# Scaling the exponentials before they are turned, in the attention of a twelve-stage block kernel

## The chip, the cores and the metric

The kernel runs on one core of one Trainium2 chip. The metric is the device time of one execution in microseconds; a kernel is judged by the median of its runs. Engines are called PE (TensorE), ACT (ScalarE), DVE (VectorE), POOL (GpSimd) and SP (the queue that issues most DMA transfers).

## The reference, cut to what matters

Two stacks of layers run one after the other on 512 latent tokens of width 1024 (the second stack also has 256 context tokens). Three layers hold a softmax attention with heads of 64 values:

```python
def fox(q, k, v, F):          # 16 heads, causal, 512 tokens: forgetting attention
    s = q @ k.T / 8 + (F_i - F_j)            # masked above the diagonal
    o = softmax(s) @ v
    return (o * silu(u @ w_z)) @ w_out
def even_mixer(...):          # layer with the "mla" attention, 8 heads, 768 keys
    y_lat = concat([a_lat, b_lat], -1) @ w_out       # b_lat = softmax(q k) v
def odd_mixer(...):           # two attentions of 8 heads each
    p = softmax(concat([s_loc, s_ctx], -1))          # "na": a window and the context, 512 keys
    d_lat = blocked_attention(qd_l, ...)             # "gqa": 768 keys
    y_lat = concat([c_lat, d_lat], -1) @ w_out
```

All is float32. A large product is made as three products of rounded halves (high x high, high x low, low x high), so each operand is needed as a "high" part (rounded copy) and a "low" part (the rest), and the left operand is needed with its features on the partitions.

## The kernel before, in words

Each engine runs a program of its own, in the order in which the functions `pe_...`, `act_...`, `dve_...` issue it; they are tied by counting semaphores (`A`, `V`, `B` are those of ACT, DVE and PE; `wait_ge(*V.of(name))` waits until DVE has done what is called `name`). Each engine runs its instructions strictly in this order, so an instruction that waits holds back all behind it. `X.chain()` waits for the engine's own last instruction.

An attention is a list of units: one head and one tile of 128 queries, with `nk` keys. Units go in pairs n, n+1. The three functions `pe_attention`, `act_attention` and `dve_attention` run over the pairs in a pipeline. In the iteration of pair n, PE does: the transposes of the exponentials of unit n-2 (`turned`, L902), the scores of n and n+1 (L893), the transposes of unit n-1, the transpose of the result of pair n-4 (`output`, L924), and the products of pair n-2 with the values (`values`, L917). ACT copies a turned unit from PSUM (`probs`, L955), makes the exponentials with their sum (`softmax`, L969, in the trace an ACTIVATE and a short ACTIVATION_READ_ACCUMULATOR behind it) and copies the pair's result (`out_copy`, L978). DVE copies the other turned unit (L1002; in fox and na, where a mask or bias is added to the scores, ACT copies both), inverts the two sums (L1006), takes the maxima of the next scores (L1023, behind the mask or bias, L1464 and L2937), and scales the turned results of pair n-4 by the inverse sums (`done`, L1031).

There are five such loops: fox (64 units: 16 each with 128, 256, 384 and 512 keys), mla in two groups (24 units each: 16 with 768 keys, 8 with 256), gqa (32 units, 768 keys) and na (32 units, 512 keys). In fox, at n = 0, 8, ..., 48, PE first runs a "side chunk" (`pe_chunk`, L558, 32 products with a modulation weight); at n = 48 ACT and DVE also split the next weights into high and low (L349 and L356, two instructions each), DVE between its maxima of pair 48 and those of pair 50. In the first mla group DVE runs two gating operations of another result (`beside`, L2754 and L2757) behind its maxima in each of the first six iterations.

The values product leaves a pair's result as features x tokens; `out_copy`, `output` and `done` turn it into tokens x features. After fox the gate z is made in tokens (`pe_linear_tok`), and the result is multiplied by it. Then every layer end (`pe_first_end`, `pe_second_end`) turns its input back into features (`pe_to_feat`, L710: 32 transposes, 48 in the even layer), ACT takes the high part (L729) and DVE the low part (L739), PE spreads a gate vector over the partitions (`pe_gate`, L756), and `pe_end` runs the output product (L400 to L402).

## Time and profile before

| | |
|---|---|
| median of 3 runs (lowest to highest) | 3508.91 us (3508.07 to 3514.5) |
| the profiled execution: its time, its span | 3506.47 us, 3504.7 us |
| PE busy | 3195.7 us (91% of the span) |
| DVE, ACT, POOL busy | 1706.0 us (49%), 1220.5 us (35%), 284.6 us (8%) |
| DMA | 301.32 MB, mean 86 GB/s |

The span is that of the profiled execution from its first to its last instruction. An engine's busy share is an average over all stages; it doesn't say which engine ends the waits in one of them. The attention loops lie at about 722 to 861 us (fox), 1895 to 1962 and 1996 to 2061 us (mla), 2887 to 2979 us (gqa) and 2980 to 3053 us (na).

### The profile page before, as it was taken

The numbers are of one execution on the slowest core, as the hardware profiler recorded it, in microseconds if no ns is written. First come the engines' busy times: TensorE is split into PE (matmuls) and PEld (weight loads), VectorE is DVE, ScalarE is ACT, GpSimd is POOL, SyncE is SP. The second block draws the span as 40 slices with busy tenths as digits, with TensorE's granted clock in tenths as the row PEclk, the third lists the DMA queues.
The fourth block names the chain that finished last, engine by engine and source line by source line (L and its number), as shares of the span: only waits on it lengthen the run. The fifth ranks groups of instructions, "written<-read, shape, count | busy, mean of one in ns | idle before, by whom it ended". The sixth has DMA issues, their size and how long they took to land.

```text
span 3504.7 us, 55559 instructions
## 1 busy us (share of the span) xinstructions
PE 3195.7 (91%) x23754; PEld 2597.7 (74%) x23754; DVE 1706.0 (49%) x2816; ACT 1220.5 (35%) x2195; POOL 284.6 (8%) x284
## 2 busy tenths in 40 slices
PE   6988988998999799899998789999999888889998
PEld 4767767755777687788886568888887775578886
DVE  3255435445433556667765545333334346644344
ACT  3325324346341465322224444211112425642221
POOL 0020010000002000133330000000000101000000
PEclk9999999989999999899998999999999989999999
DMA  5282222272224122132121001212121313013221
GB/s 203 92 299 88 96 97 73 99 282 77 74 81 168 59 71 75 55 109 76 63 71 41 25 1 45 74 64 72 49 72 52 92 50 72 1 44 113 96 97 72
DMA packets 164064, 301.32 MB, mean 86 GB/s; under 512 B 9606, under 2 KB 30919, under 8 KB 163561
## 3 DMA queue, kind: packets, MB, share of 16 engines
q1 hardware_dynamic: 148064, 278.71, 23.3%
q10 hardware_dynamic: 13641, 11.55, 1.0%
q0 software_dynamic: 2112, 7.50, 0.8%
q8 instruction: 187, 3.06, 0.4%
q14 instruction: 60, 0.49, 0.0%
HBM read 289.62 MB, written 6.76 MB: 85 GB/s over the span
## 4 chain that ended last, share of the span: by engine, by line
PE 76%; DVE 15%; ACT 6%; issue 1%; DMA 1%; POOL 0%; ACTq 0%; DVEq 0%; SPq 0%; POOLq 0%
PE psum L400 17%; PE psum L401 17%; PE psum L402 17%; PE psum L2278 5%; PE psum L893 4%; PE psum L917 3%; PE psum L902 3%; PE psum L558 2%; DVE weights_r L356 2%; DVE arena L816 1%; DVE x_lat L819 1%; PE psum L2342 1%; PE psum L2350 1%; DVE feat_r L739 1%; PE psum L756 1%
## 5 line engine op out<-in xcount | busy, mean ns | idle before, releaser
L356 DVE TENSOR_TENSOR weights_r<-weights,weights_r 128x2048 fp32r<-128x2048 f32 (+2 forms) x170 | 368.3, 2188 | 551.9 <-ACT weights_r L349 551.7
L400 PE MATMUL psum<-feat_r,weights_r 128*128 128x512 f32 (+1 forms) x1552 | 544.6, 351 | 14.7 <-DVE feat_r L697 12.4
L400 PE MATMUL psum<-weights_r,feat_r 128*128 128x512 f32 (+2 forms) x1344 | 531.5, 395 | 23.7 <-DVE feat_r L697 14.9
L401 PE MATMUL psum<-feat_r,weights_r 128*128 128x512 f32 (+1 forms) x1552 | 542.8, 350 | 0.0
L402 PE MATMUL psum<-feat_r,weights_r 128*128 128x512 f32 (+1 forms) x1552 | 542.0, 349 | 0.0
L402 PE MATMUL psum<-weights_r,feat_r 128*128 128x512 f32 (+2 forms) x1344 | 524.3, 390 | 0.0
L401 PE MATMUL psum<-weights_r,feat_r 128*128 128x512 f32 (+2 forms) x1344 | 524.3, 390 | 0.0
L349 ACT ACTIVATE weights_r<-weights 128x2048 fp32r<-128x2048 f32 (+2 forms) x170 | 306.5, 1825 | 600.9 <-DMA weights<-in_w_ffn_gate 224.9
L400 PEld LDWEIGHTS psum<-feat_r,weights_r 128*128 128x128 f32 x1552 | 296.1, 191 | 58.4 <-DVE feat_r L697 12.8
L402 PEld LDWEIGHTS psum<-feat_r,weights_r 128*128 128x128 f32 x1552 | 296.0, 191 | 37.9
L401 PEld LDWEIGHTS psum<-feat_r,weights_r 128*128 128x128 f32 x1552 | 296.1, 191 | 37.4
L400 PEld LDWEIGHTS psum<-weights_r,feat_r 128*128 128x128 f32 x1344 | 258.7, 192 | 75.6 <-DVE feat_r L697 15.8
L402 PEld LDWEIGHTS psum<-weights_r,feat_r 128*128 128x128 f32 x1344 | 257.6, 192 | 51.5
L401 PEld LDWEIGHTS psum<-weights_r,feat_r 128*128 128x128 f32 x1344 | 258.6, 192 | 49.0
L400 PE MATMUL psum<-weights_r,arena_r 128*128 128x512 f32 x440 | 173.5, 394 | 10.0 <-DVE arena L1834 6.2
L401 PE MATMUL psum<-weights_r,arena_r 128*128 128x512 f32 x440 | 172.1, 391 | 0.0
L402 PE MATMUL psum<-weights_r,arena_r 128*128 128x512 f32 x440 | 172.0, 391 | 0.0
L675 POOL CAST feat_r<-feat 128x512 fp32r<-128x512 f32 x76 | 49.1, 646 | 1393.5 <-ACT feat L667 1393.5
L1023 DVE TENSOR_REDUCE small<-psum 128x1 f32<-128x768 f32 (+4 forms) x176 | 121.7, 691 | 32.1 <-PE psum L893 22.4
L667 ACT ACTIVATE feat<-psum,small 128x128 f32<-128x128 f32 x304 | 109.0, 480 | 27.3 <-PE psum L636 24.2
L558 PE MATMUL psum<-weights,cond 128*32 128x512 f32 x768 | 100.5, 669 | 13.7 <-DVE feat L2496 8.6
L400 PEld LDWEIGHTS psum<-weights_r,arena_r 128*128 128x128 f32 x440 | 83.1, 189 | 30.5 <-DVE arena L1834 6.4
(472 smaller groups left out, 4587.2 us busy)
## 6 DMA issues: line engine op xcount, KB each, us to landing
weights<-in_w_mod SPq DMA_DIRECT2D x48, 2048.0 KB, 12.6
weights<-in_gla_w_in SPq DMA_DIRECT2D x24, 1024.0 KB, 7.4
weights<-in_w_ffn_gate SPq DMA_DIRECT2D x20, 1024.0 KB, 6.3
weights<-in_w_ffn_up SPq DMA_DIRECT2D x20, 1024.0 KB, 5.1
weights<-in_w_ffn_down SPq DMA_DIRECT2D x20, 1024.0 KB, 6.2
weights<-in_fox_w_in SPq DMA_DIRECT2D x16, 1024.0 KB, 6.8
weights<-in_sgu_w_in SPq DMA_DIRECT2D x12, 1024.0 KB, 6.2
weights<-in_gla_w_out SPq DMA_DIRECT2D x8, 1024.0 KB, 6.6
```

The costliest lines, as they stand in the source:

```text
L349: act.e.activation(WEI_r[:, s * SLOT + HALF:s * SLOT + HALF + n], WEI_t[:, s * SLOT:s * SLOT + n], ACT.Copy).then_inc(*A.put(("weights", c ...
L356: dve.e.tensor_tensor(WEI_r[:, s * SLOT:s * SLOT + n], WEI_t[:, s * SLOT:s * SLOT + n], WEI_r[:, s * SLOT + HALF:s * SLOT + HALF + n].bitc ...
L400: pe.e.matmul(ps, lh, rh, start=first, stop=False)
L401: pe.e.matmul(ps, lh, rl, start=False, stop=False)
L402: done = pe.e.matmul(ps, ll, rh, start=False, stop=last)
L558: done = pe.e.matmul(ps[32 * j:32 * j + 32, :], cond_at(mod, k, b), where[k][0], start=b == 0 and k < 4, stop=b == 1 and k >= 4)
L667: act.e.activation(FL_plain[:, k, t * P:(t + 1) * P], K.at[at][:, m * P:(m + 1) * P], ACT.Identity, bias=PRE_B[:, c0 + k:c0 + k + 1], scal ...
L893: done = pe.e.matmul(ps[m][:, n0:n0 + w], lt, rh, start=first, stop=last)
L902: done = pe.e.transpose(ps[:, j * P:(j + 1) * P], PR[n % 3][:, j * P:(j + 1) * P], ident)
L917: done = pe.e.matmul(ps[half, 0:P], units[m]["values"][j], PTR[m % 2][:, j * P:(j + 1) * P], start=j == 0, stop=j == last)
L1023: dve.e.tensor_reduce(NEGM[:, i:i + 1], src, AX.X, ALU.max, negate=True).then_inc(*V.put((tag, "max", n)))
L2278: done = pe.e.matmul(out_[rows, (h - heads[0]) * 64:(h - heads[0] + 1) * 64], lhsT[rows, h, :], rhs[rows] if len(rhs.shape) == 2 else rhs[ ...
```

## The change

**In the loops.** DVE no longer scales results. Behind each exponential it inverts the sum and multiplies the 128 x nk exponentials by it in place (`scaled`), and PE's transposes of that unit wait for this instead of for the exponential. The values product then leaves the final result, with features on the partitions; `out_copy` writes it straight to its place, and `output`, `done` and the extra iteration for them are gone. The four attention destinations (`to`) are now features x tokens.

**At the ends.** What comes from an attention isn't transposed any more; ACT and DVE split it row by row (`act_row`, `dve_row`: a row is 128 features x all tokens). After fox, z is made by features, and gate, high and low of row m follow each product; the gate vector's spreading moves into the z product. In the even layer four of eight rows still come over transposes, and ACT alternates between these and rows. In the odd layer there are eight rows and no transposes. `pe_end` waits row by row.

```diff
@@ pe_product: takes ks, the order of its terms; ready(k) is called ahead of term k @@
-    def pe_product(pe, c, ps, terms, names, ready=None):
+    def pe_product(pe, c, ps, terms, names, ready=None, ks=range(KT)):
...
+    def act_row(act, tag, k, high, y):
+
+        act.chain()
+        act.e.activation(high, y, ACT.Copy).then_inc(*A.put((tag, "high row", k)))
+
+    def dve_row(dve, tag, k, low, y, high):
+        dve.wait_ge(*A.of((tag, "high row", k)))
+        dve.e.tensor_tensor(low, y, high.bitcast(F32), ALU.subtract).then_inc(*V.put((tag, "row", k)))
...
@@ pe_end @@
+                def ready(k, t=t):
+                    pe.wait_ge(*V.of((tag, "row", k) if k in by_k else (tag, "feat", t, k // 4)))
...
@@ pe_attention @@
-            pe.wait_ge(*A.of((tag, "exp", n)))
+            pe.wait_ge(*V.of((tag, "scaled", n)))
...
-        def output(n):
-            pair = n // 2
-            pe.wait_ge(*A.of((tag, "out", pair)))
-            pe.e.transpose(K.at[(tag, "values", pair)][:, P:2 * P], out_t[pair % 2],
-                           ident).then_inc(*B.put((tag, "output", pair)))
...
@@ act_attention @@
-                act.wait_ge(*V.of((tag, "done", n - 6)))
+                act.wait_ge(*V.of((tag, "scaled", n - 6)))
...
+            at = (tag, "values", n // 2)
             act.wait_ge(*B.of((tag, "values", n)))
...
+            act.e.activation(units[n]["to"], K.at[at][:, 0:P], ACT.Copy).then_inc(*A.put(K.frees(A, at), (tag, "out", n // 2)))
...
@@ dve_attention @@
+        def scaled(n):
+
+            nk, total = units[n]["nk"], SUM[:, n % 6:n % 6 + 1]
+            dve.wait_ge(*A.of((tag, "exp", n)))
+            dve.chain()
+            dve.e.reciprocal(total, total).then_inc(*V.put())
+            dve.chain()
+            dve.e.tensor_scalar(PR[n % 3][:, 0:nk], PR[n % 3][:, 0:nk], total, None, ALU.mult).then_inc(
+                *V.put((tag, "scaled", n)))
...
-            dve.wait_ge(*A.of((tag, "exp", n)))
-            dve.chain()
-            dve.e.reciprocal(SUM[:, n % 6:n % 6 + 1], SUM[:, n % 6:n % 6 + 1]).then_inc(*V.put((tag, "inverse", n)))
...
-        def done(n):
...
         last = len(units)
-        for n in range(0, last + 4, 2):
-            if 2 <= n < last + 2:
+        for n in range(0, last + 2, 2):
+            if n >= 2:
+                scaled(n - 2)
+                scaled(n - 1)
                 probs(n - 2)
                 probs(n - 1)
...
@@ pe_fox: z by features, with the gate vector after its block 4 @@
-        pe_linear_tok(pe, (T, "z"), feat_tile, KT, "fox_w_in", 3072, 1024, LAT)
+        pe_linear_feat(pe, (T, "z"), "fox_w_in", 3072, 1024, [(0, 512)],
+                       after={((T, "z"), 4, 0): lambda: pe_gate(pe, ("end", 2), 0)})
...
@@ act_fox @@
+            act.e.activation(f_zs[m % 2], K.at[at], ACT.Silu).then_inc(*A.put(K.frees(A, at), (T, "z", m)))
+            act.wait_ge(*V.of((T, "gated", m)))
+            act_row(act, ("end", 2), m, f_H[:, m, :], f_qT[:, m, :])
...
@@ dve_fox @@
+            dve.e.tensor_tensor(f_qT[:, m, :], f_qT[:, m, :], f_zs[m % 2], ALU.mult).then_inc(*V.put((T, "gated", m)))
+            dve_row(dve, ("end", 2), m, f_L[:, m, :], f_qT[:, m, :], f_H[:, m, :])
...
@@ act_second_end @@
+        if i == 0:
+            act_to_feat(act, T, tiles, halves=(0,), between=lambda t: row(4 + t) if t < 4 else None)
+        else:
+            act.wait_ge(*B.of((W_, "na")))
+            for k in second_rows[1]:
+                row(k)
...
@@ dve_second_end @@
+        if i == 0:
+            dve_to_feat(dve, T, tiles, halves=(0,))
+            dve.wait_ge(*B.of((T, "turned")))
+        for k in second_rows[i]:
+            y, high, low = second_row(i, k)
+            dve_row(dve, T, k, low, y, high)
```

**The order on the engines.** DVE in the gqa loop before, from the maxima of one pair to the scaling of an older one:

```order
1563 L1023 TENSOR_REDUCE small<-psum 128x1 x2
1564 L1002 COPY feat<-psum 128x768
1565 L1006 RECIPROCAL small<-small 128x1 x2
1566 L1023 TENSOR_REDUCE small<-psum 128x1 x2
1567 L1031 TENSOR_SCALAR arena<-psum,small 128x64 x2
```

And DVE at the same place now:

```order
1749 L1027 TENSOR_REDUCE small<-psum 128x1 x2
1750 L997 RECIPROCAL small<-small 128x1
1751 L999 TENSOR_SCALAR feat<-feat,small 128x768
1752 L997 RECIPROCAL small<-small 128x1
1753 L999 TENSOR_SCALAR feat<-feat,small 128x768
1754 L1009 COPY feat<-psum 128x768
```

Two scalings over 768 elements stand ahead of the copy of the turned unit and of the maxima; two small ones behind the maxima are gone.

ACT from the last pair of the mla attention to the gates of the even layer's end, before:

```order
805 L955 ACTIVATE arena<-psum 128x256
806 L978 ACTIVATE arena<-psum 128x128
807 L729 ACTIVATE feat_r<-psum 128x4x128 x12
808 L765 ACTIVATE arena<-psum 128x512 x4
809 L349 ACTIVATE weights_r<-weights 128x2048 x2
```

And now:

```order
819 L976 ACTIVATE arena<-psum 128x128
820 L721 ACTIVATE feat_r<-psum 128x4x128
821 L739 ACTIVATE feat_r<-arena 128x768
822 L721 ACTIVATE feat_r<-psum 128x4x128
823 L739 ACTIVATE feat_r<-arena 128x768
824 L721 ACTIVATE feat_r<-psum 128x4x128
825 L739 ACTIVATE feat_r<-arena 128x768
826 L721 ACTIVATE feat_r<-psum 128x4x128
827 L739 ACTIVATE feat_r<-arena 128x768
828 L721 ACTIVATE feat_r<-psum 128x4x128 x2
829 L767 ACTIVATE arena<-psum 128x512 x4
```

Six of twelve high parts from PSUM became four longer ones from SBUF, which stand between the others.

DVE from the last unit of the na attention to the next weights in the odd layer's end, before:

```order
1717 L1031 TENSOR_SCALAR arena<-psum,small 128x64 x4
1718 L739 TENSOR_TENSOR feat_r<-psum,feat_r 128x4x8x16 x4
1719 L739 TENSOR_TENSOR feat_r<-psum,feat_r 128x4x128 x4
1720 L747 TENSOR_TENSOR small<-mod_cols,param_cols 128x8
1721 L681 SCALAR_TENSOR_TENSOR small<-mod_cols,param_cols 128x8
```

And now:

```order
1911 L997 RECIPROCAL small<-small 128x1
1912 L999 TENSOR_SCALAR feat<-feat,small 128x512
1913 L743 TENSOR_TENSOR feat_r<-arena,feat_r 128x512 x8
1914 L749 TENSOR_TENSOR small<-mod_cols,param_cols 128x8
1915 L682 SCALAR_TENSOR_TENSOR small<-mod_cols,param_cols 128x8
```

The low parts stay eight instructions of 512 elements, ahead of the gate vector (L749) for which PE waits; they read SBUF now and no transposes stand ahead of them.

## Rows read from the trace of the kernel before

**Rows 1.** The page's chain of work that ended last, shares of the span by engine

```profile
PE 76%; DVE 15%; ACT 6%; issue 1%; DMA 1%; POOL 0%; ACTq 0%; DVEq 0%; SPq 0%; POOLq 0%
```

**Rows 2.** Timeline of one gqa pair: start and length in us, engine, line, what

```profile
2900.84 0.90 ACT L969 ACTIVATE feat<-psum,small 128x768 f32<-128x768 f32 x1
2901.64 0.19 ACT L969 ACTIVATION_READ_ACCUMULATOR feat<-psum,small 128x1 f32 x1
2902.26 0.87 PE L902 MATMUL psum<-const,feat 128*128 128x128 f32 x6
...
2904.24 0.43 DVE L1006 RECIPROCAL small<-small 128x1 f32<-128x1 f32 x2
...
2906.37 0.90 ACT L969 ACTIVATE feat<-psum,small 128x768 f32<-128x768 f32 x1
```

**Rows 3.** Timeline of one na pair

```profile
3015.16 0.69 ACT L969 ACTIVATE feat<-psum,small 128x512 f32<-128x512 f32 x1
...
3015.42 0.69 DVE L1023 TENSOR_REDUCE small<-psum 128x1 f32<-128x512 f32 x1
...
3015.75 0.19 ACT L969 ACTIVATION_READ_ACCUMULATOR feat<-psum,small 128x1 f32 x1
...
3016.24 0.66 PE L902 MATMUL psum<-const,feat 128*128 128x128 f32 x4
```

**Rows 4.** Timeline of one fox pair with 512 keys

```profile
847.84 0.69 ACT L969 ACTIVATE x_ctx<-psum,small 128x512 f32<-128x512 f32 x1
...
848.91 0.66 PE L902 MATMUL psum<-const,x_ctx 128*128 128x128 f32 x4
```

**Rows 5.** Timeline of one pair of the first mla group

```profile
1908.62 2.02 DVE L1023 TENSOR_REDUCE small<-psum 128x1 f32<-128x768 f32 x2 [0.40 <-PE psum L893]
...
1910.61 0.90 ACT L969 ACTIVATE feat<-psum,small 128x768 f32<-128x768 f32 x1
...
1911.38 0.69 DVE L2754 TENSOR_TENSOR feat<-feat,arena 128x512 f32<-128x512 f32 x1
...
1912.03 0.87 PE L902 MATMUL psum<-const,feat 128*128 128x128 f32 x6
```

**Rows 6.** Timeline in fox behind the side chunk of n = 48

```profile
822.96 4.48 DVE L356 TENSOR_TENSOR weights_r<-weights,weights_r 128x2048 fp32r<-128x2048 f32 x2
...
825.69 1.11 PE L902 MATMUL psum<-const,x_ctx 128*128 128x128 f32 x4
```

**Rows 7.** Groups by line and form on DVE: count, busy us, mean ns

```profile
L691 DVE TENSOR_SCALAR arena<-x_lat,small 128x1024 f32<-128x1024 f32 x32 | 24.1, 754 | 1.1
...
L2129 DVE TENSOR_SCALAR arena<-arena 128x128 f32<-128x128 f32 x6 | 1.7, 283 | 0.0
```

**Rows 8.** Timeline of PE from fox's z product to its output product

```profile
904.99 0.39 PE L402 MATMUL psum<-weights_r,feat_r 128*128 128x512 f32 x1
...
916.11 0.77 PE L400 MATMUL psum<-weights_r,feat_r 128*128 128x512 f32 x1
```

**Rows 9.** Timeline of the even and the odd layer's end

```profile
2060.85 0.60 DVE L1031 TENSOR_SCALAR arena<-psum,small 128x64 f32<-128x64 f32 x2 [1.12 <-PE psum L924]
2061.51 4.32 PE L710 MATMUL psum<-const,feat 128*128 128x128 f32 x24 [0.70 <-DVE arena L1031]
...
2071.43 5.45 PE L756 MATMUL psum<-const,small 128*128 128x128 f32 x32 [2.98 <-DVE small L747]
...
3062.05 2.05 PE L756 MATMUL psum<-const,small 128*128 128x128 f32 x16 [2.32 <-DVE small L747]
```

**Rows 10.** Timeline of PE where gqa ends and na begins

```profile
2979.79 0.33 PE L924 MATMUL psum<-const,feat 128*128 128x128 f32 x1 [0.38 <-ACT feat L978]
...
2983.48 1.11 PE L902 MATMUL psum<-const,feat 128*128 128x128 f32 x4 [2.29 <-ACT feat L969]
```

**Rows 11.** Windows in na: stretch, us, busy us of PE, PEld, DVE, ACT, POOL, PEclk, DMA, GB/s

```profile
2994.62:3048.05 53.43, 44.74 (x429) 32.72 (x429) 39.68 (x105) 39.34 (x92) 0.00 (x0) 1.00 0.01 2
...
2983.00:2993.00 10.00, 8.74 (x44) 6.12 (x44) 3.35 (x9) 4.83 (x12) 0.00 (x0) 0.50 0.00 0
```

More of the change, by code:

```diff
@@ L699, in dve_low, with pe_to_feat @@
                                 ALU.subtract).then_inc(*V.put((pre, "feat", t)))
-    def pe_to_feat(pe, tag, y, tiles):
+    def pe_to_feat(pe, tag, y, tiles, halves=(0, 1)):
         pe.wait_ge(*A.of((tag, "in")))
         pe.wait_ge(*V.of((tag, "in")))
-        for h in range(2):
+        for h in halves:
             for t in tiles:
@@ L777, in pe_end @@
                 ends = [("weights", c)] if t == tiles[-1] else []
-                pe_product(pe, c, ps, [(feat_tile(k, t), where[k]) for k in range(KT)], [(tag, n0, t)] + ends)
+                def ready(k, t=t):
+                    pe.wait_ge(*V.of((tag, "row", k) if k in by_k else (tag, "feat", t, k // 4)))
+                pe_product(pe, c, ps, [(src(k, t), where[k]) for k in ks], [(tag, n0, t)] + ends, ready, ks)
                 if n0 and beside[j] is not None:
@@ L972, in out_copy @@
         def out_copy(n):
-            pair = n // 2
+            at = (tag, "values", n // 2)
             act.wait_ge(*B.of((tag, "values", n)))
-            if pair >= 2:
-                act.wait_ge(*B.of((tag, "output", pair - 2)))
             act.chain()
-            act.e.activation(out_t[pair % 2], K.at[(tag, "values", pair)][:, 0:P],
-                             ACT.Copy).then_inc(*A.put((tag, "out", pair)))
+            act.e.activation(units[n]["to"], K.at[at][:, 0:P], ACT.Copy).then_inc(*A.put(K.frees(A, at), (tag, "out", n // 2)))
         last = len(units)
-        for n in range(0, last + 4, 2):
+        for n in range(0, last + 2, 2):
             if att_side(n, sides):
                 act_side(act)
-            if 2 <= n < last + 2:
+            if n >= 2:
                 probs(n - 2)
@@ L1023, in softmax @@
             dve.e.tensor_reduce(NEGM[:, i:i + 1], src, AX.X, ALU.max, negate=True).then_inc(*V.put((tag, "max", n)))
-        def done(n):
-            pair = n // 2
-            at = (tag, "values", pair)
-            dve.wait_ge(*B.of((tag, "output", pair)))
-            for m in (n, n + 1):
-                dve.chain()
-                dve.e.tensor_scalar(units[m]["to"], K.at[at][:, P + 64 * (m % 2):P + 64 * (m % 2) + 64],
-                                    SUM[:, m % 6:m % 6 + 1], None,
-                                    ALU.mult).then_inc(*V.put(K.frees(V, at), (tag, "done", m)))
         last = len(units)
-        for n in range(0, last + 4, 2):
-            if 2 <= n < last + 2:
+        for n in range(0, last + 2, 2):
+            if n >= 2:
+                scaled(n - 2)
+                scaled(n - 1)
                 probs(n - 2)
@@ L2725, in program @@
     m_att = [FEAT_t[:, 6144 + n * 768:6912 + n * 768] for n in range(4)] + [ar(3072, 768)]
-    m_out = [ar(3840 + n * P, P) for n in range(2)]
     M_ = ("mla",)
@@ L3152, in pe_second_end @@
             pe_gate(pe, T, v)
-        pe.wait_ge(*V.of((T, "feat")))
-        pe_end(pe, T, name, tiles, ("preffn", i))
+        pe_end(pe, T, name, tiles, ("preffn", i), ks=list(range(KT)) if i == 0 else second_rows[1], by_k=second_rows[i])
         pe_ffn(pe, i, tiles)
```

157 lines of the change are left out of this document (79 added, 78 removed).

## The prediction

> **What bounds the kernel now.** I read the page's chain first: three quarters of the end time hang on PE [rows 1]. The change touches five attention loops and three layer ends, so what counts is which wait ends last inside one pair. In gqa [rows 2] the first exponential of a pair starts at 2900.84 and its accumulator row ends at 2901.64 + 0.19 = 2901.83. PE turns that unit at 2902.26, and the next pair's exponential starts at 2906.37: 5.53 us a pair. Between them PE does the next scores (they must stand behind the transposes in its program), then the second unit's transposes, ACT copies these and only then makes the next exponential. So it is one ring: exponential, transposes, scores, transposes, copy, exponential. From the exponential's end to the transposes only 0.43 us pass. In na the ring goes over the maxima; from the exponential's start to the transposes are 3016.24 - 3015.16 = 1.08 us [rows 3], and 13 pairs take 53.43 us, 4.11 each [rows 11]. Fox with 512 keys has 848.91 - 847.84 = 1.07 us there [rows 4], mla 1.42 like gqa [rows 5]. The reader is to see that nothing stands between exponential and transposes that could be taken away: PE comes nearly as soon as the exponential is done. DVE, on the other hand, is idle at that moment, and its reciprocals (0.43 us for two [rows 2]) and its scaling of results lie outside the ring.
>
> **What the change adds: a stop at DVE in the ring.** Each unit's transposes now wait for reciprocal and scaling. The parts:
>
> - A hand-over between engines: DVE's last scaling ends at 2060.85 + 0.60 = 2061.45 and PE starts at 2061.51 [rows 9]. I take 0.05 us each, from ACT to DVE and from DVE to PE.
> - Reciprocal to the next instruction that depends on it: 0.43 us for two, each 0.16, so 0.27 from start to start [rows 2].
> - The scaling itself, S. It isn't in this trace at these sizes. A multiply of SBUF by a column of scalars takes 754 ns at 1024 elements, another TENSOR_SCALAR from SBUF 283 ns at 128 [rows 7]; a line through both gives 0.49 us at 512 and 0.62 at 768. The bound from above is one element per cycle, as in a maximum over 768 from PSUM, 2.02 / 2 = 1.01 us [rows 5], or about 0.34 more at 768 and 0.25 at 512. A bound from below is no gain over the line, less 0.05. I take the line, since its upper row is the same operation with the same kinds of operands.
>
> The Trainium skill, "VectorE: DVE Perf Modes", "Mode 2×_2P — use both read ports for one tensor", says that an operation with one tensor input, SBUF on both sides, makes two results a cycle even in float32; rows 7 agree, and by that rule the sum is the one below, by the PSUM row about 20 us more.
>
> From the accumulator's end to the transposes it was 0.43 us in gqa and is now 0.05 + 0.27 + 0.62 + 0.05 = 0.99: **+0.56 us a pair** in gqa, and in mla's long pairs. In fox at 512 keys it was 0.29 (the accumulator's end is 0.78 behind the start [rows 3]) and becomes 0.37 + 0.49 = 0.86: **+0.57**; I take this for all fox pairs, as shorter units have a shorter scaling but had less slack. In na the maxima of the second unit end at 3015.42 + 0.69 = 3016.11, 0.95 behind the exponential's start and later than its accumulator; the reciprocal stands behind them in DVE's order, so the transposes come at 0.95 + 0.05 + 0.27 + 0.49 + 0.05 = 1.81 instead of 1.08: **+0.73**. Only the pair's first unit counts; the second's transposes stand behind the scores, which leave DVE over 1.5 us for it.
>
> Sum of the loops:
>
> - fox, 32 pairs. Six of the waits fall under a side chunk, which PE runs first. One (behind n = 48) is dearer: the scaling stands behind the weight splits, which end at 822.96 + 4.48 = 827.44, so PE turns at about 828.4 and not at 825.69 [rows 6], +2.7. The other 25 cost 25 x 0.57 = 14.3. Together 17.0.
> - mla: 16 long pairs x 0.56 = 9.0; 8 short ones about 0.5 each, 4.0. In the first group the two gating operations (0.69 each [rows 5], about 1.45 with gaps) now start when the maxima end, which is when the next exponential starts (1908.62 + 2.02 = 1910.64 against 1910.61), and hold DVE until 1.45 behind it, while the accumulator ends at 0.99: +0.45 five times, and 1.45 in the first iteration, where nothing else hides them: 3.7. Together 16.7.
> - gqa: 16 x 0.56 = 9.0. na: 16 x 0.73 = 11.7.
>
> Together **+54.4 us**.
>
> **What it takes away.** DVE's scaling of results and PE's `output` lie in idle time of both, so in the middle of a loop they give nothing. At a loop's end PE no longer waits for copy and transpose: 0.38 idle and 0.26 until the next scores [rows 10], about 0.65; this counts for fox, the first mla group and gqa, -2.0. At fox's end, PE went from its last z product (904.99 + 0.23) to the output product at 916.11 [rows 8]: 10.9 us. Now each row's gate, high and low run under the next row's 24 products, and the last row (Silu, multiply, copy, subtract, some 2.8 us) is ready before the first output product comes to its eighth term, 7 x 0.68 = 4.8 us in. What stays is the gate vector, about 2.0 us at PE's full clock [rows 9]: **-8.9**.
>
> In the even layer's end, the transposes no longer stand behind `output` (0.33 [rows 10]) and DVE's two scalings (0.60) with their hand-overs, so they start about 1.0 earlier, at 2060.5 [rows 9], and the first high part a good microsecond behind that, at 2061.6. ACT then alternates: six highs of 0.62 and four rows over 768, priced like the exponential's 0.90 [rows 2], 7.3 us, the sixth high ending at 2068.9. DVE takes the low parts of all six tiles first and then four rows of about 1.0, so it ends 4.7 later, at 2073.6, and the two gate vectors reach PE at about 2074.0 and not at 2071.43: **+2.6**. In the odd layer's end eight low parts stand ahead of the gate vector as before, without the lead of the transposes; PE's gate products start some 2 us before 3062.05, but behind a longer idle stretch, so at the low clock, which takes back half: **-1**, an estimate.
>
> **Sum:** 54.4 - 2.0 - 8.9 + 2.6 - 1.0 = +45.1 us. The profiled execution took 3506.5 us, 2.4 under the median of the three runs, so this gives 3551.6; against the median it would be 3554. I say 3552, 1.3% slower.
>
> **Rivals.**
>
> - *PE's clock falls.* The new waits add idle time to PE at every pair. At the start of na, after 2.29 us of idling [rows 10], the granted clock was 0.50 (1.2 GHz) for ten microseconds, and 1.00 (2.4 GHz) in the steady part with PE busy 44.74 of 53.43 us [rows 11]. With 0.73 more idle in 4.84 that busy share falls from 84% to 72%. At the low clock four transposes take 1.11 instead of 0.66 us [rows 10, 3]; scaled to all PE work of a pair, 3.44 us, of which part is hidden, a na pair is some 2 us longer: +32 if all of na stays low, and some +8 to +15 for the short pairs of fox and mla. The time would be 3570 to 3595. Against it: the gaps are under 1.5 us each and PE works in between. The Trainium skill, "TensorE: Matmul & The Clock Gate", "Part 1: The HAM clock gate (the "warmup" mystery)", says that the slow clock is the default and activity lifts it; by that rule a thinner loop can fall back, and the na start in the rows is such a case.
> - *The scaling runs at one element a cycle.* 32 long pairs x 0.34, 16 na pairs and the longer half of fox x 0.25, about 20 us more: 3572. Against it stands the 754 ns row.
> - *The ring has slack that I don't see* (half of each wait goes under something, or hand-overs are shorter): +0.25 to 0.4 a pair, 3525 to 3538.
> - *Faster: the stop at DVE is hidden.* Place: PE's transposes of each pair's first unit. If PE were still at the values product of the older pair when the scaling ends, the loops would cost nothing and the ends would give 2.0 + 8.9 - 2.6 + 1.0 = 9.3: 3497. There are 80 pairs on the ring (25 + 24 + 16 + 15 or 16), so this decides below 9.3 / 80 = 0.12 us a pair. In gqa PE's transposes follow the exponential by 0.43 us, of which PE's own older work can explain 0.38 at most if a hand-over is 0.05, and the stop is 0.99 long. Little speaks for it.
>
> **How the numbers follow.** The forecast, 3540 to 3560, has 0.5. The clock rival 0.2, slow scaling 0.08, hidden slack 0.16, the faster case 0.06. The range 3530 to 3590 takes in the bounds of S and most of the clock rival, and leaves out the faster case, the lower half of the slack case and the clock's extreme: 0.8 inside. A change under 0.2% can't be told from none here. Faster 0.06, same 0.02, slower 0.92.
>
> **What would show it.** In the changed kernel: gqa pairs of about 6.1 us (5.53 before), na 4.84 (4.11), a TENSOR_SCALAR of 0.62 us at 768, PE's transposes released by DVE and not by ACT; fox's output product straight behind the z product; PE's gate products in the even layer 14 us behind the last values product. Wrong would be unchanged pair times, or na pairs above 6 us with a granted clock of 0.50.

## The result, and the profile after

The changed kernel takes 3566.23 us (median of 4 runs, 3562.88 to 3567.17), the kernel before beside it 3508.49 us: ratio 1.0163, 95% interval 1.0148 to 1.0178, so 1.6% slower. The profiled execution took 3562.88 us with a span of 3561.1 us; before it was 3506.47 and 3504.7, so the traces differ by 56.4 us. The page after, busy time by engine and the chain that ended last (answers to [rows 1]):

```profile
PE 3196.0 (90%) x23578; PEld 2590.2 (73%) x23578; DVE 1746.7 (49%) x2814; ACT 1222.8 (34%) x2193; POOL 285.1 (8%) x284
...
PE 73%; DVE 17%; ACT 7%; issue 1%; DMA 1%; POOL 0%; ACTq 0%; DVEq 0%; SPq 0%; POOLq 0%
```

PE's busy time is as before, and DVE has won in the chain: the new work is done by an engine that was idle half the time, and the end comes later all the same. Where it comes later, by the starts of the same instructions in both traces:

| stretch | before, us | after, us | difference | in the prediction's sum |
|---|---|---|---|---|
| start to fox's first exponential | 725.77 | 726.92 | +1.15 | 0 |
| to the first z product | 135.83 | 158.49 | +22.66 | +16.35 |
| to fox's output product | 54.51 | 45.48 | -9.03 | -8.9 |
| to mla's first exponential (code unchanged) | 980.16 | 982.56 | +2.40 | 0 |
| both mla groups, to the even end's gate products | 175.16 | 191.03 | +15.87 | +18.65 |
| to gqa's first exponential (code unchanged) | 816.22 | 816.10 | -0.12 | 0 |
| to na's first exponential | 95.00 | 107.26 | +12.26 | +8.35 |
| to the odd end's output product | 81.21 | 90.56 | +9.35 | +10.7 |
| to the end (code unchanged) | 440.84 | 442.70 | +1.86 | 0 |

A gqa pair after, which answers to [rows 2] (start and length in us):

```profile
2963.92 0.90 ACT L968 ACTIVATE feat<-psum,small 128x768 f32<-128x768 f32 x1
2964.72 0.19 ACT L968 ACTIVATION_READ_ACCUMULATOR feat<-psum,small 128x1 f32 x1
2964.95 0.16 DVE L997 RECIPROCAL small<-small 128x1 f32<-128x1 f32 x1 [0.72 <-ACT feat L968]
...
2965.14 0.62 DVE L999 TENSOR_SCALAR feat<-feat,small 128x768 f32<-128x768 f32 x1
...
2965.82 0.88 PE L909 MATMUL psum<-const,feat 128*128 128x128 f32 x6 [0.41 <-DVE feat L999]
...
2969.93 0.90 ACT L968 ACTIVATE feat<-psum,small 128x768 f32<-128x768 f32 x1
```

The accumulator row ends at 2964.91. Before, PE's transposes came 0.43 us behind that; now reciprocal and scaling stand between, and PE starts at 2965.82, 0.91 behind it, released by DVE. The next pair's exponential starts 6.01 us behind this one's. A na pair, for [rows 3]:

```profile
3059.82 0.69 ACT L968 ACTIVATE feat<-psum,small 128x512 f32<-128x512 f32 x1
...
3060.07 0.69 DVE L1027 TENSOR_REDUCE small<-psum 128x1 f32<-128x512 f32 x1
...
3060.86 0.16 DVE L997 RECIPROCAL small<-small 128x1 f32<-128x1 f32 x1
3061.06 0.49 DVE L999 TENSOR_SCALAR feat<-feat,small 128x512 f32<-128x512 f32 x1
...
3061.61 0.66 PE L909 MATMUL psum<-const,feat 128*128 128x128 f32 x4 [0.64 <-DVE feat L999]
...
3064.64 0.69 ACT L968 ACTIVATE feat<-psum,small 128x512 f32<-128x512 f32 x1
```

The maxima end at 3060.76, the reciprocal starts 0.10 later, and PE comes at 1.79 us behind the exponential instead of 1.08; the pair takes 4.82 us. The scalings of mla, gqa and na (minimum, median and maximum in ns), for [rows 7]:

```profile
L999 DVE TENSOR_SCALAR feat<-feat,small x112: 352/619/4487, 1914.9 to 3105.2; 128x768 f32<-128x768 f32 x64, 128x512 f32<-128x512 f32 x32, 128x256 f32<-128x256 f32 x16
```

The two pairs above have 0.62 us at 768 keys and 0.49 at 512, as the prediction's line through two groups said. But the maximum is 4487 ns. Around it, GpSimd, DVE and PE in gqa:

```profile
2943.48 14.10 POOL L2999 TENSOR_TENSOR feat<-feat,arena 128x2048 f32<-128x2048 f32 x3 [134.62 <-DMA feat<-rpb_spans]
...
2948.72 4.49 DVE L999 TENSOR_SCALAR feat<-feat,small 128x768 f32<-128x768 f32 x1
...
2953.32 0.96 DVE L1009 COPY feat<-psum 128x768 f32<-128x768 f32 x1
...
2954.33 1.54 PE L909 MATMUL psum<-const,feat 128*128 128x128 f32 x6 [3.48 <-DVE feat L1009]
```

GpSimd's three additions over 128 x 2048 (the bias of the neighbourhood attention) happened to run under gqa. The scaling at 2948.72 lasts 4.49 us instead of 0.62, PE stands idle for 3.48 us, and its next transposes run at the low clock (1.54 us for six, 0.88 above). Two gqa pairs took 10.51 and 7.11 us in place of 6.01, 5.6 us together. Before, the additions ran under the same loop, where DVE only read PSUM and inverted sums. Its TENSOR_SCALAR from PSUM kept its 0.60 us for two beside them, and every gqa pair behind the first took 5.53:

```profile
2907.85 13.49 POOL L2997 TENSOR_TENSOR feat<-feat,arena 128x2048 f32<-128x2048 f32 x3 [133.71 <-DMA feat<-rpb_spans]
...
2912.43 0.60 DVE L1031 TENSOR_SCALAR arena<-psum,small 128x64 f32<-128x64 f32 x2
```

In fox the clock took part. Windows over the whole loop, first before, then after with two pieces of it (stretch, us, busy us of PE, PEld, DVE, ACT and POOL, PEclk, DMA share, GB/s):

```profile
725.80:861.60 135.80, 118.64 (x939) 67.63 (x939) 79.83 (x264) 83.53 (x232) 0.00 (x0) 0.91 0.57 204
```

```profile
726.90:885.40 158.50, 125.64 (x906) 68.69 (x906) 87.09 (x267) 83.29 (x232) 0.00 (x0) 0.84 0.49 175
762.00:779.00 17.00, 14.28 (x79) 7.12 (x82) 8.75 (x31) 7.71 (x26) 0.00 (x0) 0.60 0.52 193
785.80:802.00 16.20, 12.50 (x107) 6.86 (x109) 9.76 (x33) 9.24 (x29) 0.00 (x0) 1.00 0.71 251
```

At 1.00 a pair with 256 keys takes 3.35 us (2.71 before); in the piece from 762 to 779, mostly at 0.50 (1.2 GHz), 4.39 to 4.48. All in all 51.2 us of the fox loop lie at the low level, 23.9 before.

### The profile page after: what moved, and what is told of

Read it like the earlier page. It is cut to its first block, busy times and chain, and to the rows that moved or that the text cites. A ratio compares the mean times of both kernels' runs of the same rounds, so it can differ in the third digit from the quotient of the medians.

```text
span 3561.1 us, 55142 instructions
## 1 busy us (share of the span) xinstructions
PE 3196.0 (90%) x23578; PEld 2590.2 (73%) x23578; DVE 1746.7 (49%) x2814; ACT 1222.8 (34%) x2193; POOL 285.1 (8%) x284
## 4 chain that ended last, share of the span: by engine, by line
PE 73%; DVE 17%; ACT 7%; issue 1%; DMA 1%; POOL 0%; ACTq 0%; DVEq 0%; SPq 0%; POOLq 0%
PE psum L401 17%; PE psum L402 17%; PE psum L403 17%; PE psum L2282 5%; PE psum L900 4%; PE psum L909 3%; PE psum L559 2%; DVE weights_r L356 2%; DVE small L1027 1%; DVE arena L823 1%; DVE feat L999 1%; DVE x_lat L826 1%; ACT feat L968 1%; PE psum L2346 1%; PE psum L2354 1%
## 5 line engine op out<-in xcount | busy, mean ns | idle before, releaser
L401 PE MATMUL psum<-feat_r,weights_r 128*128 128x512 f32 (+1 forms) x1616 | 569.8, 353 | 15.9 <-DVE feat_r L698 12.4
L402 PE MATMUL psum<-feat_r,weights_r 128*128 128x512 f32 (+1 forms) x1616 | 567.1, 351 | 0.0
L403 PE MATMUL psum<-feat_r,weights_r 128*128 128x512 f32 (+1 forms) x1616 | 566.3, 350 | 0.0
L401 PE MATMUL psum<-weights_r,feat_r 128*128 128x512 f32 (+2 forms) x1216 | 481.6, 396 | 23.7 <-DVE feat_r L698 14.9
L402 PE MATMUL psum<-weights_r,feat_r 128*128 128x512 f32 (+2 forms) x1216 | 474.6, 390 | 0.0
L403 PE MATMUL psum<-weights_r,feat_r 128*128 128x512 f32 (+2 forms) x1216 | 474.3, 390 | 0.0
L401 PEld LDWEIGHTS psum<-feat_r,weights_r 128*128 128x128 f32 x1616 | 307.7, 190 | 62.8 <-DVE feat_r L698 12.8
L402 PEld LDWEIGHTS psum<-feat_r,weights_r 128*128 128x128 f32 x1616 | 307.9, 191 | 39.7
L403 PEld LDWEIGHTS psum<-feat_r,weights_r 128*128 128x128 f32 x1616 | 307.5, 190 | 40.3
L401 PEld LDWEIGHTS psum<-weights_r,feat_r 128*128 128x128 f32 x1216 | 234.7, 193 | 70.7 <-DVE feat_r L698 15.9
L403 PEld LDWEIGHTS psum<-weights_r,feat_r 128*128 128x128 f32 x1216 | 234.0, 192 | 46.1
L402 PEld LDWEIGHTS psum<-weights_r,feat_r 128*128 128x128 f32 x1216 | 234.9, 193 | 43.9
L401 PE MATMUL psum<-weights_r,arena_r 128*128 128x512 f32 x504 | 198.8, 394 | 10.0 <-DVE arena L1838 6.2
L402 PE MATMUL psum<-weights_r,arena_r 128*128 128x512 f32 x504 | 197.3, 391 | 0.0
L403 PE MATMUL psum<-weights_r,arena_r 128*128 128x512 f32 x504 | 197.1, 391 | 0.0
L909 PE MATMUL psum<-const,feat 128*128 128x128 f32 x544 | 86.8, 291 | 47.6 <-DVE feat L999 40.4
L401 PEld LDWEIGHTS psum<-weights_r,arena_r 128*128 128x128 f32 x504 | 95.3, 189 | 33.1 <-DVE arena L1838 6.4
```

The lines of the kernel that those rows point to most:

```text
L401: pe.e.matmul(ps, lh, rh, start=first, stop=False)
L402: pe.e.matmul(ps, lh, rl, start=False, stop=False)
L403: done = pe.e.matmul(ps, ll, rh, start=False, stop=last)
L909: done = pe.e.transpose(ps[:, j * P:(j + 1) * P], PR[n % 3][:, j * P:(j + 1) * P], ident)
```

## Experiments

All are timed beside the kernel before on the same chip; pair times are the distances of the pairs' first exponentials, medians of a loop. The kernel before took 3507 to 3511 us (medians) in each group of runs, so a difference to the changed kernel is good to a few us.

**1. No stop.** The scaling is left out (results are not normalised), PE waits for the exponential, and DVE's reciprocals go back behind its copies.

```diff
-            pe.wait_ge(*V.of((tag, "scaled", n)))
+            pe.wait_ge(*A.of((tag, "exp", n)))
```

> The changed kernel without the scaling of the exponentials: PE's transposes wait for the exponential alone, DVE makes the reciprocals behind its copies as before, nothing is normalised. What is left of the change are the shorter loop tails and the three ends. Theory 1 (the stop at DVE costs the time): pairs fall back to 5.53 us in gqa and 4.11 in na, the clock in fox is as before, and the ends show alone: about 9 us under the kernel before, 3497 to 3501. Rival (the ends or the new place of the results cost, or the clock falls for another reason): 3515 or more. If the fox clock were low here too, it is not the stop that lowers it.

3499.12 us, ratio 0.9977 (0.9964 to 0.9991). gqa 5.53, na 4.11, mla 6.57: the old pair times to the hundredth. Fox's window has the clock of before:

```profile
725.90:861.60 135.70, 115.70 (x910) 64.80 (x911) 62.48 (x203) 84.01 (x233) 0.00 (x0) 0.91 0.57 204
```

So the loops' loss hangs on the stop at DVE, the longer low clock in fox too. What is left of the change, the three ends and the shorter loop tails, gives 8.3 us by the medians, near the 9 foretold. That isn't all theirs by this trace: the start of na, in both kernels at the low level for 10.2 us, stayed at 1.00, and na's loop took 61.41 us instead of 65.40.

**2. Two columns.** The multiply takes `[:, 0:2]` instead of all keys; the rest is unscaled. This keeps hand-overs and reciprocal in the ring and takes out the length of the multiply.

> The changed kernel, but the scaling multiplies two columns instead of all keys, so the hand-overs, the reciprocal and one short instruction stay in the ring and the long multiply goes (the rest of the exponentials is left unscaled). Theory (hand-overs and multiply are additive): a multiply of two columns is some 0.22 us, so a gqa pair takes 0.40 less than 6.01, about 5.6, a na pair loses 0.27 of 4.82, about 4.55; with the pair of gqa that met GpSimd's additions cured as well, about 3525 to 3532. Rival (it is the hand-over alone that costs): pair times hardly move, above 3550.

3538.44 us (1.0095, 1.0077 to 1.0113): 6 to 13 over what I wrote. The pair times are those foretold, gqa 5.62 and na 4.56. What I had wrong was that a short scaling would be safe from GpSimd:

```profile
2935.96 13.43 POOL L2999 TENSOR_TENSOR feat<-feat,arena 128x2048 f32<-128x2048 f32 x3 [132.80 <-DMA feat<-rpb_spans]
...
2936.10 4.38 DVE L999 TENSOR_SCALAR feat<-feat,small 128x2 f32<-128x2 f32 x1
...
2940.58 0.17 DVE L997 RECIPROCAL small<-small 128x1 f32<-128x1 f32 x1
2940.78 4.16 DVE L999 TENSOR_SCALAR feat<-feat,small 128x2 f32<-128x2 f32 x1
...
2945.04 0.96 DVE L1009 COPY feat<-psum 128x768 f32<-128x768 f32 x1
```

One addition lasts 4.48 us. The first, from 2935.96, ends at 2940.44, and the scaling of two columns (228 ns elsewhere) ends at 2940.48; the second ends at 2944.91, the next scaling at 2944.94. It isn't slowed in proportion, it stands until the other is done. The reciprocal between them (0.17) and the copy from PSUM are not held. Two gqa pairs took 13.00 and 6.81 us, 8.6 too much. The Trainium skill, "SBUF — State Buffer", "Who interferes with whom", says just that: the second port pair is an exclusive lock for a whole instruction, taken by GpSimd or by a vector operation in a two-port mode, and the later one fully blocks. These rows agree, and I had left this rule out of the prediction.

**3. Scaled twice.** A second multiply of the same form directly behind the first (the exponentials are then scaled by the square).

> The changed kernel with every scaling made twice in a row (the exponentials are scaled by the square, a different result). Theory (each pair is on the ring and pays one scaling): +0.65 us a pair in gqa and mla (48 pairs with 8 short), +0.52 in na, +0.3 to 0.5 in fox's 26: about +45 us, 3611; more (3620 to 3640) if the clock falls further, as it did in two stretches of fox. Rival (part of the pairs has slack): under +30 us.

3643.31 us (1.0387, 1.0371 to 1.0402), 77 over the changed kernel, more than any of my figures. mla's long pairs took 7.61 (+0.66) and na's 5.34 (+0.52), as foretold; fox's at 512 keys 5.33 (+0.52, where I had 0.3 to 0.5). But gqa took 7.01, +1.00: there DVE's copy of the first unit's transposes stands behind four multiplies now. The collision cost 9.5 us in one pair (16.48), and 30.7 us of na fell to the low clock (10.2 in both kernels), with pairs up to 6.92; fox had 71.7 us of it. So every pair is on the ring, and the whole loss was larger than the added waits.

**4. GpSimd's additions left out** (the bias tables then lack the mask).

```diff
-            pool.e.tensor_tensor(tv, tv, rows_over(w_nam[:, kind, :], 64), ALU.add).then_inc(*G.put((W_, "bias", kind)))
+            G.mark((W_, "bias", kind))
```

> The changed kernel without GpSimd's three additions over 128 x 2048 during gqa (the neighbourhood attention then goes without its mask). In the changed kernel one DVE scaling beside them took 4.49 us and not 0.62. Theory (DVE's scaling and GpSimd's addition hinder each other in SBUF): every scaling over 768 takes 0.62 us, the two long gqa pairs (10.51 and 7.11 us) go back to 6.01, and the time falls by 5 to 6 us, to about 3561. Rival (the stall is of another origin): the long pair stays and the time within 1 us.

3556.54 us (1.0142, 1.0125 to 1.0159). The long pairs are gone, gqa's loop takes 92.91 instead of 97.47 us. The medians differ by 9.7 us; the intervals touch those of the changed kernel, so the size goes by the loop, 4.6 us net (5.6 less 1.0 that the first pair took longer).

**5. GpSimd between the scalings.** Six halves, each behind a pair's second scaling.

```diff
+            for half in range(2):
+                pool.wait_ge(*V.of(((W_, "gqa"), "scaled", 9 + 4 * kind + 2 * half)))
+                rows = slice(32 * half, 32 * half + 32)
+                pool.e.tensor_tensor(tv[:, rows, :], tv[:, rows, :], rows_over(w_nam[:, kind, :], 32),
+                                     ALU.add).then_inc(*G.put((W_, "bias", kind)))
```

> The changed kernel with GpSimd's three additions cut into six halves (128 x 1024), each of which waits for the second scaling of a gqa pair (pairs 4 to 9), so that it runs while DVE reads PSUM. All work is kept. Theory (a scaling that meets an addition stands until that addition's end, since both want the same way into SBUF): no scaling over 0.7 us, gqa pairs all 6.01, the time that of the kernel without the additions, 3556 to 3561. Rival (the additions cost through something else, such as GpSimd's traffic beside DVE's reads of PSUM): copies or maxima grow, or the time stays near 3566.

3560.99 us (1.0152, 1.0135 to 1.0169), gqa's loop 92.89 us with all the work done. GpSimd and DVE's scalings in this kernel:

```profile
2948.13 2.35 POOL L3002 TENSOR_TENSOR feat<-feat,arena 128x1024 f32<-128x1024 f32 x1 [142.07 <-DVE feat L999]
```

```profile
L999 DVE TENSOR_SCALAR feat<-feat,small x112: 352/620/623, 1912.9 to 3098.5; 128x768 f32<-128x768 f32 x64, 128x512 f32<-128x512 f32 x32, 128x256 f32<-128x256 f32 x16
```

No scaling is over 623 ns. It is a matter of when, not of how much.

**6. Scores first.** In fox and na PE makes the next pair's scores ahead of the first unit's transposes.

```diff
+            if narrow and n < last:
+                scores(n)
             if n >= 2:
                 turned(n - 2)
-            if n < last:
+            if not narrow and n < last:
                 scores(n)
```

> The changed kernel, but in fox and na (one PSUM bank a unit) PE makes the next pair's scores ahead of the first unit's transposes instead of behind them. Then PE has work while DVE scales. Theory (the stop is in the ring because PE's scores stand behind the transposes that wait for DVE): the stop is covered, na pairs go from 4.82 to 4.1 to 4.3 and fox's at 512 keys from 4.81 to about 4.4, fox's clock recovers in part; about 18 us less, 3542 to 3550. Rival (the ring closes over another engine, by DVE's order of maxima behind scalings): pairs move by less than 0.2 us, 3560 to 3566.

3537.72 us (1.0082, 1.0067 to 1.0097), 28.5 less than the changed kernel. na's pairs took 4.21 and fox's at 512 keys 4.44, 0.10 and 0.11 over the kernel before: most of the stop has gone. In this trace PE's scores start at 3040.71 while DVE scales, and the transposes follow at once:

```profile
3040.64 0.48 DVE L1001 TENSOR_SCALAR feat<-feat,small 128x512 f32<-128x512 f32 x1
...
3040.71 1.14 PE L900 MATMUL psum<-arena 64*128 64x256 f32 x8
...
3041.77 1.09 PE L909 MATMUL psum<-const,feat 128*128 128x128 f32 x8
```

With it went the added low clock of fox, 23.9 us again:

```profile
726.30:863.00 136.70, 111.75 (x900) 64.02 (x902) 85.76 (x266) 83.38 (x231) 0.00 (x0) 0.91 0.57 202
```

I had written about 18 us, with the clock recovering in part. Fox's loop became 21.3 us shorter and na's 10.8; in gqa the collision with GpSimd cost more than in the changed kernel (a pair of 12.17 us).

**7. New order on three engines.** PE: scores(n), values(n - 4), both transposes; ACT: first exponential, copies, second exponential; DVE: scaling, maximum, scaling, maximum (fox and na only).

> The changed kernel, and in fox and na the order of all three engines is changed: PE makes scores, the values product of two pairs ago, then both units' transposes; ACT makes the first exponential ahead of the copies; DVE takes the maxima between the two scalings. Theory (most of a narrow pair is waiting, and an order that overlaps three pairs removes it): na pairs 3.6 to 3.9 us, fox's at 512 keys 3.8 to 4.0, 30 to 35 us less than the changed kernel, 3530 to 3537. Rival (ACT or the clock becomes the bound): na above 4.3.

3530.56 us (1.006, 1.0045 to 1.0075). The first exponentials of two na pairs start at 3042.22 and 3045.97: 3.75 us a pair where the kernel before takes 4.11, with the scaling in it. Fox at 512 keys takes 3.85, but 37.5 us of fox are at the low clock again, and its loop isn't shorter than in experiment 6 (132.25 to 132.34 us).

**8. The same order without the change.** The kernel before, with its `output` put first in PE's iteration.

> The kernel before (scaling of results behind the values product) with the same new order of PE, ACT and DVE in fox and na. It tells what the order is worth without the change, and so what the change costs where the stop can be covered. Theory: na pairs go from 4.11 to 3.3 to 3.5 us, fox's at 512 keys from 4.33 to 3.8; 20 to 26 us under the kernel before, 3482 to 3488. Rival (the order only covers the scaling and gives nothing without it): within 3 us of the kernel before.

3603.35 us (1.027, 1.0255 to 1.0286), 115 us over what I wrote. na:

```profile
3074.01 0.28 ACT L984 ACTIVATE feat<-psum 128x128 f32<-128x128 f32 x1
...
3074.35 0.33 PE L924 MATMUL psum<-const,feat 128*128 128x128 f32 x1 [2.56 <-ACT feat L984]
...
3074.60 1.95 PE L893 MATMUL psum<-arena 64*128 64x256 f32 x8
...
3076.57 0.43 DVE L2955 TENSOR_TENSOR psum<-psum,feat 128x256 f32<-128x256 f32 x1 [1.26 <-PE psum L893]
```

PE's `output` heads the iteration and waits for ACT's copy of the values, the last thing in ACT's iteration; the scores stand behind it, the maxima behind those, and a pair takes 7.07 us (median; 6.01 to 7.74). I built a new ring with my placing of one transpose, so this run says nothing about what the order would be worth without the change. That stays open. It does show what the change makes simple: without `output` there is nothing to place.

**9. All three covers.** Experiments 5 and 7, and mla's gating operations ahead of the maxima.

```diff
+            if n // 2 < len(beside):
+                beside[n // 2](dve)
             if not narrow and n < last:
                 softmax(n)
```

> The changed kernel with the new order in fox and na, GpSimd's halves between scalings in gqa, and in the first mla group the two gating operations of a pair ahead of the next maxima instead of behind them. Theory (three separate costs, each with its own place): against the kernel with the new order alone (3530.6) gqa loses its long pairs (-6 to -7) and mla's five pairs of 7.51 us go to 6.95 (-3 to -4): 3519 to 3523. Rival (the gating hides nothing where it is put, because it then delays the maxima): mla pairs stay at 7.5. What is left over the kernel before is then the stop in the wide loops, which no order covers.

3518.69 us (1.0023, 1.0013 to 1.0033). In the first mla group all long pairs behind the first take 6.95 (five took 7.51 in the changed kernel), gqa's loop 92.01. Against the kernel before, by the traces: the two mla groups take 12.6 us more, gqa's loop 6.9 and the even end 1.7; from fox's first exponential to mla's 6.6 us are won, in na's loop 9.0. So the loss that is left lies in the long loops, where each pair still pays the stop; but 5.5 of the 12.6 us are the first intervals of the two groups (9.80 and 10.05 us against 7.77 and 6.57), with 6.8 us at the low level in each group. Fox still has 37.5 us at the low level.

**10. Scaling in halves** in mla and gqa, on top of 5 and the gating's new place, without the new order.

```diff
+            parts = [(0, nk)] if nk <= NMAX else [(0, 384), (384, nk)]
+            for c0, c1 in parts:
...
+                if nk > NMAX and j == 3:
+                    pe.wait_ge(*V.of((tag, "scaled", n)))
```

> The changed kernel with its own order, GpSimd's halves and mla's gating ahead of the maxima, and in mla and gqa at 768 keys the scaling cut in two of 384, PE's first three transposes waiting for the first alone. Theory (the wait is for the end of the multiply, so its first part is enough to start): 0.42 instead of 0.62 us ahead of the transposes, the second multiply hidden but for what 3 transposes (0.43 us) don't cover; 0.19 less a pair, gqa 5.82 and mla 6.76; in all 3566 - 6 - 3.5 - 6 = 3550 (3547 to 3555). Rival (the longer occupation of DVE delays the copies and the second unit): pairs unchanged or longer, 3556 or more.

3562.91 us (1.0147, 1.0131 to 1.0163), and gqa pairs of 6.20, not 5.82: the rival. One pair:

```profile
2961.74 0.88 DVE L1003 TENSOR_SCALAR feat<-feat,small 128x384 f32<-128x384 f32 x2
...
2962.21 1.00 PE L911 MATMUL psum<-const,feat 128*128 128x128 f32 x6 [0.21 <-DVE feat L1003]
...
2962.91 0.87 DVE L1003 TENSOR_SCALAR feat<-feat,small 128x384 f32<-128x384 f32 x2
...
2963.89 0.96 DVE L1013 COPY feat<-psum 128x768 f32<-128x768 f32 x1
...
2964.90 0.88 PE L911 MATMUL psum<-const,feat 128*128 128x128 f32 x6 [0.20 <-DVE feat L1013]
```

PE does start sooner (0.21 idle instead of 0.41), but DVE is now at the second unit's halves until 2963.78 when the first unit's transposes wait to be copied; the copy starts at 2963.89 and the second unit's transposes wait for it. The limit moved from DVE's wait to DVE's queue. mla's steady pairs gained 0.07 (6.88), but the two intervals in which each group goes over to short units lost 1.9 us or more (6.20 and 5.08 in the second group, 5.86 and 3.46 in the changed kernel).

**11. Hybrid.** mla and gqa scale results on tokens as before and turn them back to features with one more transpose and copy a pair, two more iterations a loop; fox and na as in 7.

```diff
+        for n in range(0, last + 6, 2):
+            if n >= 6:
+                back(n - 6)
```

> Scaling of the exponentials only in fox and na, with the new order that covers it; in mla and gqa the results are scaled behind the values product as before, then turned back to features by one more transpose and copy a pair, placed in gaps of PE and ACT. The ends are those of the changed kernel. Theory: mla and gqa pairs return to 6.57 and 5.53 us (or up to 0.1 over, if the second transpose is not all in the gap), na stays at 3.75, the fox end keeps its 9 us: 3493 to 3503, under both kernels. Rival (the transpose back lies on the ring, 0.27 a pair and a hand-over): pairs 0.3 longer, some 3510.

3512.87 us (1.0006, 0.9996 to 1.0017): no difference to the kernel before, and 10 us over what I wrote. gqa took 5.73 and mla 6.57 to 6.68, where experiment 12, without the transpose back, has 5.53 and 6.57; so it is partly on the ring. From the first exponential of the first mla group's last pair to the next group's first, 42.45 us pass (39.47 in experiment 7). Some 5 us lay ahead of mla, in code that is that of experiment 7; no experiment shows why.

**12. By features only where it is covered.** mla, gqa and the even end are those of the kernel before; fox and na as in 7, the odd end turns gqa's four groups and takes na's four rows.

```diff
-    second_rows = [[4, 5, 6, 7], [4, 5, 6, 7, 0, 1, 2, 3]]
+    second_rows = [[], [0, 1, 2, 3]]
```

> Scaling of the exponentials only in fox and na, with the new order that covers it there; mla, gqa and the even layer's end are the kernel before (results scaled on tokens, then transposed). Fox's end goes row by row as in the changed kernel; the odd end turns gqa's four groups and takes na's four rows. Theory (the change pays where the stop is covered and costs where PE waits for it): na's loop 56.7 instead of 65.4 us (-8.7), fox's loop +1.5 and its end -9, mla and gqa pairs 6.57 and 5.53 with no collision with GpSimd: about 16 us under the kernel before, 3490 to 3499. Rival (what the hybrid lost beyond its pairs, some 15 us, did not lie in its two extra iterations per wide loop): over 3503.

3501.41 us (median of 11) against 3509.12 (15 runs): 0.9974, 0.9963 to 0.9984. It is 7.7 us faster than the kernel before, half of what I wrote. na's loop took 57.54 instead of 65.40 us. But what follows na's loop takes 461.1 us to the end, 456.7 both before and in experiment 7: 2.7 of these 4.5 us lie ahead of the first output product of the mixed odd end, the other 1.8 behind it, in code that is the same in both kernels. And mla's first exponential comes 3.4 us earlier than before, where I had 7.5. The trace says where the 4 us went: fox's loop is 1.5 us longer, as I wrote, and its end gives 9.0, but between the loop's last pair and the first z product lie 6.48 us instead of 5.09 (6.48 in experiment 7 too, so it comes with the new order), and the unchanged code from the output product to mla took 2.5 us longer.

## Why the prediction was right, and what it mis-sized

The mechanism was right: PE's transposes waited for a stop at DVE in a ring that had no slack. Experiment 1 shows it by taking the stop away, experiment 6 by covering it. The time lay in the range, the forecast's 3540 to 3560 was passed by 6. The sum was 45.1 us, the traces say 56.4. The range had room for part of the clock rival. It was luck that the collision with GpSimd, which the prediction doesn't have, fitted into it as well, and that mla, 2.8 under its term, made up for part of it. Term by term:

- *The scaling S*: 0.62 and 0.49 us, as taken. The rival of one element a cycle fell.
- *Reciprocal to the next instruction*: I took 0.27 from start to start; it was 0.19 to 0.20. So gqa got +0.48 a pair and not +0.56, na +0.71 and not +0.73; na's loop and end are 1.35 under the sum.
- *mla*: long pairs +0.38, not +0.56, and short ones +0.21, not +0.5. 0.08 is again the reciprocal; 0.10 came back between the two units' transposes (3.39 us before, 3.29 now). A pair with gating took +0.94 against 1.01, but only because two errors cancel: the stop is 0.18 shorter, and the gating on top of it costs 0.56 (7.51 to 6.95, as experiment 9 shows) and not 0.45. DVE in the first iterations, where the reciprocal starts only when the gating is over:

```profile
1920.35 2.02 DVE L1027 TENSOR_REDUCE small<-psum 128x1 f32<-128x768 f32 x2 [2.23 <-PE psum L900]
1922.41 0.69 DVE L2757 TENSOR_TENSOR feat<-feat,arena 128x512 f32<-128x512 f32 x1
1923.13 0.69 DVE L2760 TENSOR_TENSOR feat<-feat,arena 128x512 f32<-128x512 f32 x1
1923.93 0.16 DVE L997 RECIPROCAL small<-small 128x1 f32<-128x1 f32 x1
1924.13 0.62 DVE L999 TENSOR_SCALAR feat<-feat,small 128x768 f32<-128x768 f32 x1
```

  The second group's first interval was 8.71 us (6.57 before), with 3.4 us at the low level; in experiments 4 and 5, with the same code there, it was 7.01 and had none. Without that mla would lie still further under its term.

- *gqa*: pairs below the term, yet the stage 3.9 above it. What failed is the sentence that costs the pair alone. The scaling met GpSimd's additions (5.6 us here, 8.6 in experiment 2, 9.5 in one pair of experiment 3), and the prediction says nothing of what POOL does under that loop.
- *Fox*: 6.3 above the term. At the full clock pairs grew by 0.64 (256 keys), 0.55 (384) and 0.48 (512), about as summed. The pairs with 128 keys, most of them at the low level in both kernels, grew by 0.35. The rest is the clock rival, in one loop: 27 us more at the low level. Four intervals there, of 4.48, 4.39, 8.57 and 5.97 us, are 5.6 us over their like at the full clock (3.35, 3.35, 6.28 as before with its side chunk, and 4.81). I had 8 to 15 us for fox and mla inside a rival that I gave 0.2 as a whole, and nothing in the sum. For na I had feared a fall because PE's busy share would drop from 84% to 72% (3.44 of 4.84 us is 71%); it dropped to 70%, 41.92 of 60.00 us, and the clock held at 1.00 in steady state. Behind n = 48 the interval was 8.95 against 5.70, +3.25 (2.7 forecast).
- *Fox's end*: -9.03 against -8.9. The output product (L401 with `arena_r`) stands straight behind the z product, where before 10.9 us lay between [rows 8]:

```profile
885.41 0.50 PE L401 MATMUL psum<-feat_r,weights_r 128*128 128x512 f32 x1
...
930.66 0.39 PE L403 MATMUL psum<-feat_r,weights_r 128*128 128x512 f32 x1
930.89 0.39 PE L401 MATMUL psum<-weights_r,arena_r 128*128 128x512 f32 x1
```

- *The even end*: +2.6 was too much; from the last mla pair's exponential to the gate products it is +1.7, though my 2.6 already included the earlier start of the transposes. That start came (1.0 earlier relative to the last values product), and DVE's four rows stand last as said, but ACT's steps of a high and a row took 1.36 us, not 1.52. The gate products came 12.2 us behind the end of the last values product, where I had named 14:

```profile
2092.64 4.51 PE L711 MATMUL psum<-const,feat 128*128 128x128 f32 x24 [0.38 <-ACT arena L976]
...
2100.67 3.55 DVE L743 TENSOR_TENSOR feat_r<-arena,feat_r 128x768 fp32r<-128x768 f32 x4
...
2104.48 6.57 PE L758 MATMUL psum<-const,small 128*128 128x128 f32 x32 [7.33 <-DVE small L749]
```

- *The odd end*: counted from the transposes of the last pair's first unit, the gate products started 2.95 us earlier. But PE had been idle for 6.66 us, the granted clock was 0.50 from 3110.3 to 3120.6, and they took 3.78 us instead of 2.05 [rows 9]. Up to the first output product, which still starts at the low level, -1.3 is left (-1 estimated):

```profile
3114.97 3.78 PE L758 MATMUL psum<-const,small 128*128 128x128 f32 x16 [6.66 <-DVE small L749]
```

- *Unchanged stretches*: +5.3 in all. Single executions of one kernel lay up to 14 us apart here. The stretch from fox's output product to mla's first exponential, the same code in every kernel here, took 979.7 to 991.4 us in the fourteen traces. So I read nothing into them.

45.1 + 6.3 (fox) - 0.1 (fox end) - 2.8 (mla, even end) + 3.9 (gqa) - 1.35 (na, odd end) + 5.3 (unchanged) = 56.4.

## What to carry to other kernels

Before work is moved to an idle engine, ask whether another engine's next instruction will wait for it, and what stands behind that instruction in its program; where independent work is put ahead of the wait (experiment 6), the move is nearly free, and where it isn't, as in mla and gqa here, each pair pays the stop. Whether the wide loops' scores, which take two banks of PSUM, could go ahead of it too, no run here tests. Ask also whether GpSimd runs long instructions at that time: a short multiply on DVE from SBUF to SBUF can last as long as one of them (experiment 2), while reads of PSUM went on beside it. And split an instruction to start its reader earlier only when its own engine has time for the extra part (experiment 10).

## What the hardware showed that I had not expected

A DVE multiply of two columns took 4.38 us beside a GpSimd addition and ended 0.04 us after it, and the wait stands in the trace as length of the DVE instruction and not as idle time. Reciprocals of one column and reads of PSUM passed. TensorE's clock fell to 0.50 in fox, at 765.4 and at 840.5 among others, without a long pause ahead of it: in the 6.8 us at 1.00 before the one fall PE was busy for 5.35 us and no gap was over 0.88 us, in the 10.2 us before the other it was busy for 8.11. In na it held 1.00 from 3040 to 3100 with PE busy for 41.92 of 60.00 us, a smaller share. Why the one fell and the other not, these runs don't tell.
